# Sample state in the chunk loop, sample values in four column strips, and a new order inside the attention steps

## The reference

```python
def diff_attn_core(q, k, v, q_pos, k_pos, lam):
    s = jnp.einsum("bqhd,bkhd->bhqk", q, k) * (DA_QK ** -0.5)
    s = jnp.where(k_pos[None, :] <= q_pos[:, None], s, -jnp.inf)
    p = jax.nn.softmax(s, axis=-1).reshape(b, DA_HEADS, 2, tq, tk)
    w = p[:, :, 0] - lam * p[:, :, 1]            # two maps per head
    return jnp.einsum("bhqk,bkhd->bqhd", w, v)

def wkv7_scan(state0, r, w, k, v, a, b):
    def step(S, inp):
        Sa = jnp.einsum("bhij,bhj->bhi", S, a_t)
        S = S * w_t[:, :, None, :] + Sa[..., None] * b_t[:, :, None, :] + v_t[..., None] * k_t[:, :, None, :]
        return S, jnp.einsum("bhij,bhj->bhi", S, r_t)
```

## Time and profile before

| | |
|---|---|
| Median of 3 runs | 3040.86 us (3040.59 to 3041.26) |
| Profiled execution | 3035.79 us, span of the trace 3034.1 us |
| PE, PEld busy | 2831.4 us (93%), 2597.7 us (86%) |
| DVE, ACT, POOL busy | 1360.5 us (45%), 658.5 us (22%), 249.5 us (8%) |
| Chain that ended last | PE 87%, DVE 9%, ACT 2% |
| The dense line L1639 in that chain | 69% |
| Mean granted clock of TensorE | 0.961 |

### The profile page before, as it was taken

The page is one execution under the profiler, slowest core; times in us unless marked ns, Lnnn a source line. Parts: engine busy times, 40 slices in busy tenths (PEclk is TensorE's granted clock), DMA queues, the critical chain, the costliest instruction groups (busy, mean ns, idle before and its releaser), DMA issues.

```text
span 3034.1 us, 51486 instructions
## 1 busy us (share of the span) xinstructions
PE 2831.4 (93%) x21353; PEld 2597.7 (86%) x21353; DVE 1360.5 (45%) x1360; ACT 658.5 (22%) x967; POOL 249.5 (8%) x250
## 2 busy tenths in 40 slices
PE   6999999999999999979987999458999999999998
PEld 6999999999999999963435998127999999999998
DVE  4332233134664887674553443565444322331333
ACT  4111111012212223322322232011222111110123
POOL 1000000000011231120003442000000000000000
PEclk8999999999999999979998999767999999999999
DMA  3111111112333456685442000003311111111112
GB/s 105 44 46 49 49 41 49 49 41 71 103 122 121 123 190 204 198 318 176 135 122 64 3 3 8 19 16 126 118 49 45 45 49 49 41 49 49 42 42 76
DMA packets 264284, 246.70 MB, mean 81 GB/s; under 512 B 17364, under 2 KB 212784, under 8 KB 264000
## 3 DMA queue, kind: packets, MB, share of 16 engines
q1 hardware_dynamic: 247040, 184.09, 20.2%
q0 software_dynamic: 16896, 60.33, 5.4%
q10 hardware_dynamic: 192, 0.07, 0.0%
HBM read 204.62 MB, written 39.82 MB: 81 GB/s over the span
## 4 chain that ended last, share of the span: by engine, by line
PE 87%; DVE 9%; ACT 2%; issue 1%; DMA 0%; DVEq 0%; POOL 0%; SPq 0%; POOLq 0%; ACTq 0%
PE ps L1639 69%; PE ps L1846 3%; PE ps L1942 1%; PE ps L1957 1%; PE ps L1962 1%; PE ps L1662 1%; PE ps L2110 1%; DVE rstd L1552 1%; PE ps L1864 1%; PE ps L1683 1%; DVE small L1420 1%; PE ps L1969 1%; PE ps L1891 1%; PE ps L1879 1%; PE ps L1803 1%
## 5 line engine op out<-in xcount | busy, mean ns | idle before, releaser
L1639 PE MATMUL ps<-h_hi,w_hi 128*128 128x344 f32 x3072 | 991.7, 323 | 10.3 <-DVE w_lo L1144 10.3
L1639 PE MATMUL ps<-h_lo,w_hi 128*128 128x344 f32 x3072 | 980.6, 319 | 0.0
L1639 PE MATMUL ps<-h_hi,w_lo 128*128 128x344 f32 x3072 | 980.1, 319 | 0.0
L1639 PEld LDWEIGHTS ps<-h_hi,w_hi 128*128 128x128 f32 x3072 | 577.7, 188 | 25.9 <-issue 19.8
L1639 PEld LDWEIGHTS ps<-h_lo,w_hi 128*128 128x128 f32 x3072 | 578.0, 188 | 2.1 <-issue 1.9
L1639 PEld LDWEIGHTS ps<-h_hi,w_lo 128*128 128x128 f32 x3072 | 577.9, 188 | 0.0
L1639 PE MATMUL ps<-ff_hi,w_hi 128*128 128x344 f32 x1056 | 337.1, 319 | 0.0
L1639 PE MATMUL ps<-ff_lo,w_hi 128*128 128x344 f32 x1056 | 336.6, 319 | 0.0
L1639 PE MATMUL ps<-ff_hi,w_lo 128*128 128x344 f32 x1056 | 336.2, 318 | 0.0
L794 ACT ACTIVATE w_hi<-w_stage 128x1024 fp32r<-128x1024 f32 x194 | 203.8, 1051 | 479.9 <-PE ps L1639 479.9
L1144 DVE TENSOR_TENSOR w_lo<-w_stage,w_hi 128x1024 fp32r<-128x1024 f32 x194 | 239.2, 1233 | 138.0 <-ACT w_hi L794 103.7
(11 more groups left out here) (393 smaller groups left out, 3280.1 us busy)
## 6 DMA issues: line engine op xcount, KB each, us to landing
w_stage<-in_ffn_up SPq DMA_DIRECT2D x176, 256.0 KB, 3.1
key_ring<-in_cache_k SPq DMA_DIRECT2D x128, 256.0 KB, 3.0
value_ring<-in_cache_v SPq DMA_DIRECT2D x128, 256.0 KB, 2.9
w_stage<-in_w_in SPq DMA_DIRECT2D x84, 256.0 KB, 3.3
w_stage<-in_ffn_down SPq DMA_DIRECT2D x80, 256.0 KB, 2.9
gate_save<-tmp POOLq DMA_DIRECT2D x16, 516.0 KB, 4.5
gate_ring<-gate_save POOLq DMA_DIRECT2D x16, 516.0 KB, 4.3
x_save<-x_res POOLq DMA_DIRECT2D x8, 516.0 KB, 2.9
```

The lines of the kernel that those rows point to most:

```text
L1639: last = mm(dense[s][:, j], w[w0][:, k0 + k, :], r[:, k, j * CH:(j + 1) * CH], start=(k == 0 and n == 0), stop=(k == nk - 1 and n == 2))
```

## The change

1. The sample state moves into the chunk loop. There are no diagonals and no PE products for it any more: SP stores the five vectors of all samples to a small buffer in HBM, and loads each row back, spread over 64 partitions, into a ring of two (`rowring`). DVE does one of the 36 steps behind each `ck_y_level` sum from the second on. The last step of each head writes to `ysam`, which is copied to `CUM` behind the loop. POOL stores the sample state ahead of the prompt's.
2. The four value products of a group go to four column strips, partitions 32j to 32j+3 of bank 7, each of which sums over the four groups of a sample. ACT moves all 128 partitions, and `turn_sums` multiplies them with a constant (`strip_sum`) that adds the strips. Bank 7 is cleared once in the third softmax piece.
3. On PE `turn_sums` and `weight_values` go ahead of the turns of the same step, behind the scores of the next.
4. On DVE `maxima(step + 1)` and `sample_out` go ahead of the merge of the step.

```diff
 # SP, behind the loads of the sample state
+            for done in ("kk_back", "b_back", "kp_back", "r_back"):
+                sp.wait_ge(*ev.at(done, 16 * HP))
+            sp.wait_ge(*ev.at("w_sample", 1))
+            for n, src in enumerate((KKn[:, :, NP:NT], wsam, Bf[:, :, NP:NT], Kf[:, :, NP:NT], Rf[:, :, NP:NT])):
+                for x, q in enumerate(halves):
+                    sp.dma_start(row_save[n, x].rearrange("h j b -> j h b"), src[q]).then_inc(ev["rows_saved"], 16)
+            sp.wait_ge(*ev.at("rows_saved", 16 * 10))
+            for i in range(5 * HP):
+                if i >= 2:
+                    sp.wait_ge(*ev.at("row_used", i - 1))
+                for x, q in enumerate(halves):
+                    sp.dma_start(rowring[q, i % 2], row_save[i % 5, x, i // 5].unsqueeze(0).broadcast_to([64, 64, NS]))\
+                        .then_inc(ev[f"row_back{i % 2}"], 16)
...
 # DVE, third softmax piece
+                    in_turn(v.memset(PS[:, 7, :], 0.0))
+                    in_turn(v.tensor_tensor(strip_sum, K("ident_stack")[:, 0:HP], K("ident_stack")[:, 32:32 + HP], ALU.add))
...
 # DVE, attention
             for step in range(STEPS):
+                if step + 1 < STEPS:
+                    maxima(step + 1)
+                for b in range(NS):
+                    if FILL_STEP[4 * b + 3] == step - 1:
+                        sample_out(b)
                 dve.wait_ge(*ev.at("probs_made", 2 * step + 2))
...
-                if step + 1 < STEPS:
-                    maxima(step + 1)
                 if step < 3:
                     sample_softmax(step)
-                for b in range(NS):
-                    if FILL_STEP[4 * b + 3] == step - 1:
-                        sample_out(b)
...
 # DVE, level_sums
                 in_turn(v.tensor_tensor(y, y, heads8(DY_PS), ALU.add).then_inc(ev["ck_y_level"], 1))
+                if 1 <= level(c, l) - 1 <= 9 * HP:
+                    state_step(level(c, l) - 2)
...
+            ROW_OF = [0, 0, 1, 2, 2, 3, 3, 4, 4]
+            def state_step(k):
+                h, part = divmod(k, 9)
+                S, n = St[:, h], 5 * h + ROW_OF[part]
+                row = rowring[:, n % 2].rearrange("p j b -> p b j")
+                if part in (0, 2, 3, 5, 7):
+                    dve.wait_ge(*ev.at(f"row_back{n % 2}", 32 * (n // 2 + 1)))
+                if part == 0:
+                    in_turn(v.tensor_tensor(stm, S, row, ALU.mult).then_inc(ev["row_used"], 1))
+                if part == 1:
+                    in_turn(v.tensor_reduce(sa, stm, AX, ALU.add))
...
 # DVE, behind the loop: the block of the sample state goes
+            in_turn(v.tensor_copy(CUM[:, :, NP:NT], ysam))
             dve.wait_ge(*ev.at("wkv_trans", 1))
             in_turn(v.tensor_copy(wfin[0:64], ps4(6, 0, P)[0:64]).then_inc(ev["wkv_made"], 1))
...
 # PE, weight_values and turn_sums
-                    last = mm(PS[0:HP, 7, :], VIEW_W[:, b, g, :], vring[:, f % 2, j, :], start=(g == 0), stop=(g == PAGES - 1))
+                    last = mm(PS[32 * j:32 * j + HP, 7, :], VIEW_W[:, b, g, :], vring[:, f % 2, j, :],
+                              start=(f % 4 == 0), stop=(f % 4 == 3))
...
-                    last = mm(PS[:, 7, h:h + 1], osum[0:HP, h * P:(h + 1) * P], K("ident")[0:HP, h:h + 1], start=True, stop=True)
+                    last = mm(PS[:, 7, h:h + 1], osum[:, h * P:(h + 1) * P], strip_sum[:, h:h + 1], start=True, stop=True)
...
 # PE, attention
                     scores(step + 1)
                 if step == 2:
                     sample_sums()
+                for b in range(NS):
+                    if FILL_STEP[4 * b + 3] == step - 1:
+                        turn_sums(b)
+                for f in range(4 * NS):
+                    if FILL_STEP[f] == step:
+                        weight_values(f)
                 pe.wait_ge(*ev.at("w_ready", step + 1))
...
                 last.then_inc(ev["o_done"], 1)
-                for b in range(NS):
-                    if FILL_STEP[4 * b + 3] == step - 1:
-                        turn_sums(b)
-                for f in range(4 * NS):
-                    if FILL_STEP[f] == step:
-                        weight_values(f)
...
 # PE, behind the loop
-            for h in range(HP):
-                pe.wait_ge(*ev.at("row_diag", 5 * h + 5))
-                if h:
-                    pe.wait_ge(*ev.at("state_new", h))
-                for n in range(5):
-                    last = mm(PS[:, n, :], K("block_ones"), dg[:, n].rearrange("p b j -> p (b j)"), start=True, stop=True)
-                last.then_inc(ev["rows_made"], 1)
-            pe.wait_ge(*ev.at("state_new", HP))
```

More of the change, by code:

```diff
@@ L138 @@
     [("tok_clear", 1), ("par_moved", 2), ("lam_prod", 1), ("x_scaled", 9), ("rope_done", 8), ("z_place", ZT), ("neg_max", 32),
-     ("ck_lt", NC), ("row_diag", 5 * HP), ("yb_full", HP), ("merge_full", KT), ("y_moved0", 5)],
-    [("x_low", 9), ("vsam_made", HP), ("z_last", ZT), ("w_ready", 32), ("ck_aka", NC), ("state_new", HP), ("yb_split", HP),
+     ("ck_lt", NC), ("yb_full", HP), ("merge_full", KT), ("y_moved0", 5)],
+    [("x_low", 9), ("vsam_made", HP), ("z_last", ZT), ("w_ready", 32), ("ck_aka", NC), ("yb_split", HP),
      ("merged", KT)],
@@ L147 @@
     [("norm_inverse", HP), ("ck_s", NC + 1)],
-    [("x_trans", 18), ("kv_trans", 16), ("scores_done", 32), ("ck_blocks", NC), ("rows_made", HP), ("o_spread", HP), ("y_trans", 9)],
+    [("x_trans", 18), ("kv_trans", 16), ("scores_done", 32), ("ck_blocks", NC), ("o_spread", HP), ("y_trans", 9)],
     [("par_trans", 1), ("rstd_rows", 2), ("lam_sums", 1), ("s_sum", 1),
@@ L239, in build @@
         tok = small[:, 40:49]
+        strip_sum = small[:, 52:56]
         span = at("mid_decay", HP * NC)[:, :].rearrange("p (h c) -> p h c", h=HP)
@@ L341, in build @@
         St = at("state", 2 * KT * P, base)[:, :].rearrange("p (h b j) -> p h b j", h=HP, b=NS)
-        dg = cols("row_diag", 8, 5 * 512).rearrange("p (v b j) -> p v b j", v=5, b=NS)
-        stm = cols("state_tmp", 11, 512).rearrange("p (b j) -> p b j", b=NS)
+        rowring = at("row_ring", 2 * 512, arena + 33 * TILE)[:, :].rearrange("p (s j b) -> p s j b", s=2, b=NS)
+        stm = work(512).rearrange("p (b j) -> p b j", b=NS)
+        ysam = work(HP * NS).rearrange("p (h b) -> p h b", h=HP)
         sa = small[:, 8:16]
@@ L357, in build @@
             for name in ("q", "k", "r", "v", "kk", "b", "kp", "cum")]
+        row_save = nc.dram_tensor("row_save", (5, 2, HP, 64, NS), F32).ap()
         gd_save = nc.dram_tensor("gd_save", (P, NT), F32).ap()
@@ L750, in _ @@
                     first_masks(c + 1)
-            pool.wait_ge(*ev.at("wkv_made", 1))
-            pool.dma_start(A["wkv_prompt"][0, 0].rearrange("(h two) i j -> i h two j", two=2),
-                           wfin[0:64].rearrange("i h (two j) -> i h two j", two=2)).then_inc(ev["wkv_stored"], 16)
             pool.wait_ge(*ev.at("state_new", HP))
@@ L758, in _ @@
                     .then_inc(ev["state_stored"], 16)
+            pool.wait_ge(*ev.at("wkv_made", 1))
+            pool.dma_start(A["wkv_prompt"][0, 0].rearrange("(h two) i j -> i h two j", two=2),
+                           wfin[0:64].rearrange("i h (two j) -> i h two j", two=2)).then_inc(ev["wkv_stored"], 16)
             pool.wait_ge(*ev.at("ya_split", HP))
@@ L1024, in _ @@
                         act.wait_ge(*ev.at("value_used", 4 * b + 4))
-                        sc.activation(osum[0:HP, :], PS[0:HP, 7, :], ACT.Copy).then_inc(ev["osum_moved"], 1)
+                        sc.activation(osum, PS[:, 7, :], ACT.Copy).then_inc(ev["osum_moved"], 1)
             act.wait_ge(*ev.at("o_sample", NS))
@@ L1488, in next_state @@
                 in_turn(v.tensor_tensor(new, new, bc(span[:, :, p:p + 1], 64), ALU.mult).then_inc(ev["ck_s"], 1))
+            ROW_OF = [0, 0, 1, 2, 2, 3, 3, 4, 4]
[9 more added lines that the diff above has]
+                    in_turn(v.tensor_reduce(sa, stm, AX, ALU.add))
+                if part == 2:
+                    in_turn(v.tensor_tensor(S, S, row, ALU.mult).then_inc(ev["row_used"], 1))
+                if part == 3:
+                    in_turn(v.tensor_tensor(stm, sa.unsqueeze(2).broadcast_to([P, NS, 64]), row, ALU.mult).then_inc(ev["row_used"], 1))
+                if part == 4:
+                    in_turn(v.tensor_tensor(S, S, stm, ALU.subtract))
+                if part == 5:
+                    in_turn(v.tensor_tensor(stm, Vf[:, h, NP:NT].unsqueeze(2).broadcast_to([P, NS, 64]), row, ALU.mult)
+                            .then_inc(ev["row_used"], 1))
+                if part == 6:
+                    in_turn(v.tensor_tensor(S, S, stm, ALU.add).then_inc(ev["state_new"], 1))
+                if part == 7:
+                    in_turn(v.tensor_tensor(stm, S, row, ALU.mult).then_inc(ev["row_used"], 1))
+                if part == 8:
+                    in_turn(v.tensor_reduce(ysam[:, h, :], stm, AX, ALU.add))
             blocks(0)
```

(2 more changed lines are left out.)

18 lines of the change are left out of this document (removed).

## The result

The changed kernel takes 3048.2 us (median of 7 runs, 3043.3 to 3053.7), the kernel before in the same session 3040.6 (7 runs, 3036.2 to 3041.3): ratio 1.0029, 95% interval 1.0018 to 1.0041. It is slower by 7.6 us; forecast was 16.5 us faster. The profiled span grew from 3034.1 to 3046.5 us.

The account below looks back on a forecast made before the run. PE (93% busy) was taken as the bound, with attention a ring through four engines. Terms -66.9 + 10 + 5 (attention at full clock) + 35 (clock), say -16.5 us, made 3040.86 into 3024.4 us; range 2988 to 3050.

Parts of the forecast that it names:

- The clock term: Attention: PE, about half busy, is granted 1.2 GHz for 0.6 of the time; +35 us, bounds 0 and 65.
- The tail: End of attention, last exponentials to the sums over o_squares: 20.6 us shrink to 10.1, so -10.5 us.
- State block: Behind the chunk loop: the sample state leaves the path, first cum_y sum starts near 1898.2 instead of 1965.06; -66.9 us.
- Chunk loop: 36 added DVE state steps lengthen the loop by +10 us, bounds +4 and +25.
- First four steps: Start of attention: the third softmax piece now stands ahead of the maxima of step 4; +2 us, bounds 0 and 4.
- Strips: Attention's value products: a group in four column strips takes 1 to 2 us instead of 3.6, hidden either way.
- The ring at full clock: Attention steps 4 to 31: links in series, 5.6 us narrow to 11.7 wide, 236.5 us instead of 223.5; +13.
- all at 1.2 GHz: Attention wholly at half clock: +0.7 us per narrow step, +3.7 per wide, 58 us, 65 with the ends.
- (c): Rival: low clock in nearly all attention, +65, and strided steps with POOL's lock, +20 in the loop; 3064 us, chance 0.13.
- (a): Rival: in attention, bursts of scores and fills keep PE at 2.4 GHz; 2989 us, chance 0.17.
- (b): Rival: in attention, strips don't run beside each other, fills stay 3.6 us, clock near 1.0; 2998 us, chance 0.12.
- (d): Rival: in the chunk loop, rows arrive late from SP, DVE waits with PE behind it; 3044 us, chance 0.05.

Follow-up runs that it names:

- the run kept busy: Changed kernel with three more zero-weight products of 512 columns in each group of value products (one group in two in the last four steps): 3025.9 us.

## Why the prediction was wrong

Two terms of the sum were mis-sized, and they turn the sign. The clock term was put at +35 us and was about +51: the step behind it that failed is the price of the low clock for the outputs and the turns. The tail was put at -10.5 us and gave -2.6: two fills that wait for their pages now stand ahead of the last turns. The mechanism (a ring in series, an idler PE, a lower clock) was right.

The attention part, from runs with the state part in all of them:

| us, median | maxima behind the merge | maxima ahead |
|---|---|---|
| strips, value products behind the outputs | 2955.5 | 3096.9 |
| strips, value products ahead of the turns | 3003.6 | 3048.2 |
| no strips, products behind the outputs | 2983.4 | not run |
| no strips, products ahead of the turns | not run | 3029.9 |

`sample_out` on DVE stands ahead of the merge in the rows with the products ahead of the turns and behind it in the others.

Step by step:

- **State block, -66.9.** Measured -66.5; the first sum waits for the load named there, 5.0 us behind the start of the copy instead of the 4.6 assumed.
- **Chunk loop, +10.** Measured +9.9 (279.0 - 269.1), for the reason given. What PE waits in the loop for the DVE step behind level 4 (us in total, times, longest), before and after:

```profile
PE ps L1975 <- DVE chunk_work L1512: 2.1, 7, 0.6
...
PE ps L2007 <- DVE chunk_work L1563: 8.9, 7, 1.5
```

  Taken to idle places, the steps cost 7.3 us less. Strided rows take 1.09 us (estimate 1.05), and up to 1.90 where one of POOL's instructions is ahead of them. The Trainium skill, "SBUF — State Buffer", section "SBUF: two separate sides", has such pairs exclude each other; these numbers agree with it, for both engines.
- **First four steps, +2.** Measured +2.9.
- **Strips.** 1.04 us for a group at full clock and 1.89 at half, the two ends of 1 to 2. That they are hidden in the new order was right but for the end of attention. The Trainium skill, "TensorE: Matmul & The Clock Gate", section "Part 3: Packing small matmuls — row/col tiling", has a speedup of 2.38 for three strips. Taken for the group as it stands, that gives 3.60 / 2.38 = 1.5 us as an estimate and not the 1.3 of the prediction; the sum did not use either. The measured 1.04 decides.
- **The ring at full clock, +13.** Held: in the run kept busy, rings without a finished sample are 6.67, 7.77, 8.69, 9.58, 10.57 and 11.71 us; the line drawn from 5.6 to 11.7 gives 6.6, 7.6, 8.7, 9.7, 10.7 and 11.7. No run has strips of 1.04 us, this order and full clock throughout, so the +13 itself is these rings added up. The run kept busy as a whole needs 266.9 us for steps 4 to 31, 43 more than before, and some 31 of them are its long fourth rings; `sample_out` was priced at 3 in all.
- **The clock, +35: the first term that failed, in its size.** What the slower clock added can be read off the products of the ring alone, steps 4 to 31. Before (scores, outputs, turns):

```profile
1360.97:1584.50 223.53, 37.60 (x172) 14.85 (x172) 0.98 0.49 152
1360.97:1584.50 223.53, 36.95 (x265) 31.90 (x264) 0.98 0.49 152
1360.97:1584.50 223.53, 20.57 (x132) 14.02 (x132) 0.98 0.49 152
```

and after (the same three):

```profile
1368.72:1656.37 287.65, 56.73 (x172) 21.82 (x172) 0.69 0.39 116
1368.72:1656.37 287.65, 60.35 (x250) 52.90 (x250) 0.69 0.39 116
1368.72:1656.37 287.65, 30.66 (x132) 21.16 (x132) 0.69 0.39 116
```

  The second number is PE's busy time: 95.1 us became 147.7, +52.6. That is near what is left of +64.1 without the ring's +13, 51 (15 records of outputs are missing after, so +52.6 is some 3 us too low). The share of the time at half clock was forecast well: 0.6, and a granted 0.69 is 62%. The price of "all at 1.2 GHz", 58 us, was too low. It gave a narrow ring 0.7 us, with nothing for its outputs and next to nothing for its turns. Split by the same lines as an estimate, the forecast's 35 us are 18 for scores, 14 for outputs and 3 for turns; the rows above have 19.1, 23.4 and 10.1. So the scores were priced right, and outputs and turns were short. And in a ring in series all three count: with four key blocks the rings are 9.73 to 9.85 us after against 7.77 in the run kept busy, 2.0 more, where the line through 0.7 and 3.7 gives 1.7 even with all of it at half clock; at half clock outputs, scores and turns take 2.08, 2.08 and 1.12 us there and at full 1.16, 1.13 and 0.66, which is +79%. On 95.1 us that makes 75 us as an estimate if all is at 1.2 GHz, and 0.62 of it 47. The strips are a part of this: with the same orders and whole-array fills the granted clock is 0.92.
- **The tail, -10.5: the second.** Measured -2.6. The sum let the turns follow the merge; but the fills 30 and 31 stand ahead of the last turns now, and wait for their pages:

```profile
1661.35 1.04 PE L1877 MATMUL ps<-value_ring,s_weights 128*4 128x512 f32 x8 [1.81 <-DMA value_ring<-in_cache_v]
1665.00 1.89 PE L1877 MATMUL ps<-value_ring,s_weights 128*4 128x512 f32 x8 [2.60 <-DMA value_ring<-in_cache_v]
1666.82 1.97 PE L1917 MATMUL ps<-const,probs 128*128 128x128 f32 x8
```

  The late page was in the earlier trace rows and was quoted; what was missed is that the move puts it onto the path of the turns. The merge is over at 1661.3, so the turns are 5.5 us late. The rest is the clock again, granted 0.50 there: these turns take 1.97 us instead of 1.09 and the outputs behind them 3.76 instead of 2.02.
- **The sum.** Clock +16 and tail +8 on a forecast of -16.5 make +7.5; measured +7.6. That it closes to 0.1 us is luck: the single terms are not known that well. The time is inside the range given, and on the side that had 0.15.
- **Rivals.** (c) named the place and the point of turning: the clock term past some 52 us with the loop at +10. That was worked out with the tail at -10.5; with the tail at -2.6 the sign turns at 44, and 51 is past it. (a) is refuted by 0.69. (b), no strips in effect, could be built: 3029.9 us, not 2998. Its clock was right (0.92), its rings lacked the wait of every fourth step, about 4.5 us by 7. (d) did not happen.

Why the orders cost so much together is in the table. With strips, the maxima ahead cost 141 us when the fills stand behind the outputs and 45 when they stand ahead of the turns; the fills ahead cost 48 with the maxima behind and give back 49 with the maxima ahead. The second order repairs the first, and with strips neither is worth having. How much of the 141 is the series and how much the clock was not taken apart.

## What to carry to other kernels

Price an exchange of order in a hand-off ring by asking which two links ran beside each other before it; here one line moved put the merge and the next scores in series, and PE, with shorter fills to bridge the wait, was granted half clock for 62% of the time. The length of a filler costs only where something waits behind it: shorter fills gained 28 us where the scores waited for them, and cost 18 us where PE waited anyway, so time each part of a change by itself, and in both orders. When a slower clock is a risk, price it on the busy time of every product in the ring, not on the links that overlap today.

## What the runs showed of the hardware

Four products into four column strips of PE run beside each other: a group of four spans 1.04 us at full clock against 3.60 on the whole array, a factor of 3.5, and 1.89 at the low clock. Adding products of zeros made a kernel faster by 22 us where PE was 68% busy (granted 0.69, then 0.93), and slower by 30 where it was 69% to 75% busy at a granted clock of 0.82 to 1.00 (from step 8 on; in steps 4 to 7 it was 80% and 0.65). The busy share alone does not give the clock: steps 8 to 19 of that second kernel, 69% to 74% busy, were granted 1.00, and steps 4 to 11 of the changed one, 71% to 73% busy, 0.57 to 0.60 (a product at the low clock counts as busy for longer). Weight loads slow with the clock as products do: the outputs' loads have a median of 333 ns after and 192 before. A step of DVE with two inputs in SBUF and an instruction of POOL do not run beside each other: started second, DVE's takes up to 1.90 us (2.08 once) instead of 1.09, and POOL's 1.86 instead of 1.28. The start of attention varies by 5 us over these traces; the runs of the kernel before alone spread by as much (3036.2 to 3041.3).
